# Delta rule of a two-block layer: VectorE instead of GpSimd makes the masked factors of the inverse's levels

## The reference, cut to what matters

```
def step(s, inp):
    r_t, w_t, k_t, v_t, a_t, b_t = inp
    sa = jnp.einsum('bhvk,bhk->bhv', s, a_t)
    s = s * w_t[:, :, None, :] + sa[..., None] * b_t[:, :, None, :] + v_t[..., None] * k_t[:, :, None, :]
    y = jnp.einsum('bhvk,bhk->bhv', s, r_t) if emit else None
    return s, y
```

## Time and profile before

| | |
|---|---|
| median of 3 runs | 3859.14 us (3858.52 to 3877.39) |
| profiled execution | 3855.31 us, of which span 3853.2 us |
| busy over the span | PE 87%, VectorE 62%, ScalarE 49%, POOL 21% |
| stage `rwmix` in the trace | from 785 to 1296 us |
| busy in the stage, 784 to 1292 us | PE 415.5, VectorE 293.5, POOL 301.3, ScalarE 281.6 us of 508 |
| `X` on POOL (line 1428) | 200 instructions, 142.2 us busy, 730 ns each |
| granted TensorE clock in the stage | 0.96 of full speed |

### The profile page before, as it was taken

One profiled execution on the slowest core, in us unless ns is written; L12 is line 12 of the kernel. 1 busy time (PEld: TensorE's weight loads), 2 busy tenths in 40 slices (PEclk: granted clock), 3 DMA queues, 4 the chain that ended last, 5 costly groups with the idle time before them and its releaser, 6 DMA issues. The chain is left out here.

```text
span 3853.2 us, 90173 instructions
## 1 busy us (share of the span) xinstructions
PE 3336.3 (87%) x33247; PEld 2257.5 (59%) x33247; DVE 2376.5 (62%) x4427; ACT 1907.1 (49%) x2993; POOL 823.9 (21%) x1095
## 2 busy tenths in 40 slices
PE   4899799768887597889989989998699999697699
PEld 0899798756766475633323333332377778576577
DVE  1688688845566575537767767776485753076631
ACT  0576567645555343217757767775322221076520
POOL 4000000045566200522212222221222323100000
PEclk6999899879999798989999999999899999898899
DMA  8354444432232437669799999950734223455342
GB/s 317 78 165 160 163 128 142 167 84 59 58 81 62 162 101 252 118 237 321 229 296 349 339 358 343 284 132 6 238 87 120 66 82 104 113 148 128 117 167 77
DMA packets 574272, 639.75 MB, mean 166 GB/s; under 512 B 121312, under 2 KB 485536, under 8 KB 570768
## 3 DMA queue, kind: packets, MB, share of 16 engines
q1 hardware_dynamic: 548576, 564.59, 46.1%
q0 software_dynamic: 25216, 69.34, 7.4%
q10 hardware_dynamic: 48, 0.05, 0.0%
HBM read 489.41 MB, written 161.74 MB: 169 GB/s over the span
## 5 line engine op out<-in xcount | busy, mean ns | idle before, releaser
L2606 PE MATMUL routed_p_gu<-routed_fixed,routed_x 128*32 128x512 f32 x3840 | 569.3, 597 | 0.0
L2606 PE MATMUL routed_p_gu<-moe_exp_w,routed_x 128*32 x1280 | 568.3, 597 | 0.7 <-DVE routed_fixed L2721 0.7
L2721 DVE COPY routed_fixed<-moe_exp_w 128x1024 f32 x640 | 400.8, 683 | 37.5 <-DMA moe_exp_w<-in_exp_w_up_dram 30.4
L2660 ACT COPY routed_fixed<-moe_exp_w 128x1024 f32 x320 | 333.7, 1046 | 134.1 <-PE routed_p_y L2621 83.7
L544 PE MATMUL front_ps<-front_a_high,front_w_high 128*128 128x320 f32 (+1 forms) x1120 | 364.4, 325 | 16.3 <-DVE front_w_low L797 13.3
L544 PE MATMUL front_ps<-front_a_high,front_w_low 128*128 128x320 f32 (+1 forms) x1120 | 355.3, 317 | 0.0
L544 PE MATMUL front_ps<-front_a_low,front_w_high 128*128 128x320 f32 (+1 forms) x1120 | 355.2, 317 | 0.0
L2606 PEld LDWEIGHTS routed_p_gu<-moe_exp_w,routed_x 128*32 128x32 f32 x1280 | 134.9, 110 | 353.6 <-issue 353.6
L2673 ACT COPY routed_fixed<-routed_wd 128x1024 f32 x240 | 235.2, 1043 | 130.1 <-PE routed_p_gu L2606 95.0
L3610 PE MATMUL pre_ps<-pre_a_high,pre_w_high 128*128 128x512 f32 x720 | 287.4, 399 | 14.0 <-ACT pre_xb L3763 7.0
L2621 PE MATMUL routed_p_y<-routed_wd,routed_hT 128*32 x640 | 290.5, 597 | 5.2 <-ACT routed_fixed L2673 5.2
(11 more groups left out here) (541 smaller groups left out, 7466.3 us busy)
## 6 DMA issues: line engine op xcount, KB each, us to landing
moe_exp_w<-in_exp_w_gate_dram SPq DMA_DIRECT2D x64, 1024.0 KB, 11.7
moe_exp_w<-in_exp_w_up_dram SPq DMA_DIRECT2D x64, 1024.0 KB, 15.8
routed_wd<-in_exp_w_down_dram SPq DMA_DIRECT2D x64, 1024.0 KB, 14.7
front_wt<-in_w_in_dram SPq DMA_DIRECT2D x70, 512.0 KB, 4.4
mod_w<-in_w_mod_dram SPq DMA_DIRECT2D x24, 1024.0 KB, 18.2
pre_wt<-in_w_in_dram SPq DMA_DIRECT2D x44, 512.0 KB, 3.9
rw_abrk<-front_rb SPq DMA_DIRECT2D x64, 320.0 KB, 4.9
rwmix_src<-rw_abrk SPq DMA_DIRECT2D x80, 192.0 KB, 2.5
```

Source lines behind the costliest of these rows:

```text
L2606: op = nc.tensor.matmul(p_gu[spot(s), :], x[:, b % 2, k, spot(s)], w, start=(k == 0), stop=(k == KD - 1))
L2660: nc.scalar.copy(fixed[:, place_of(b, c), 0, :], wgu[:, bass.ds(e % WS, 1), c * D:(c + 1) * D].rearrange("p o n -> p (o n)"))\
L2721: op = nc.vector.tensor_copy(fixed[:, place_of(b, c), s - 1, :], wgu[:, bass.ds(es[s] % WS, 1), c * D:(c + 1) * D].rearrange("p o n -> p ( ...
```

## The change

`level(l)`, the multiply of `at` by the mask of level l, is issued by VectorE instead of POOL. Levels 1 to 3 follow in slot `masked`, behind `cc` and one drain; levels 4 and 5 follow VectorE's `W` of `w1` and of `w2`. PE's wait for `x{l}` is now on VectorE's count. POOL keeps `TT`, `faded` and `gate`, and no longer waits for `w1` and `w2`. The instruction's shape, operands and number (200) stay; PE's and ScalarE's instructions and their order stay.

```
-            out = ["keys", "at", "bk", "cc"] + norm[0:1]
+            out = ["keys", "at", "bk", "cc", "x1", "x2", "x3"] + norm[0:1]
             for l in range(1, LEVELS + 1):
-                out += [f"w{l}"] + norm[l:l + 1]
+                out += [f"w{l}"] + ([f"x{l + 3}"] if l < 3 else []) + norm[l:l + 1]
...
-                    PO.wait(pe, by_pool[u], n, f"x{l}")
+                    DV.wait(pe, by_vector[u], n, f"x{l}")
...
+                def level(l):
+                    nc.vector.tensor_tensor(X[u][:, l % 3], at[u][:], consts["rw_mask"][:, MASK_LEVEL + l], ALU.mult)\
+                        .then_inc(by_vector[u], 1)
...
                     op.then_inc(by_vector[u], 1)
+                    dve.drain()
+                    for l in range(1, 4):
+                        level(l)
...
+                    if p in ("w1", "w2"):
+                        level(int(p[1]) + 3)
...
-                    for l in range(1, 4):
-                        level(l)
-                elif p in ("w1", "w2"):
-                    PE.wait(pool, products[u], n, p)
-                    level(int(p[1]) + 3)
```

## The result

The changed kernel takes 3973.24 us (median of 4 runs, 3966.3 to 3978.53) against 3860.43 us before (4 runs, 3858.52 to 3877.39). The ratio is 1.0288, with a 95% interval of 1.027 to 1.0307: 113 us slower. Forecast was 3914 us (59 over the profiled execution before) and a range up to 3945. So the direction was right, and the loss is nearly twice the forecast one and outside the range.

A forecast was written before the change was run, and what follows sets the result against it. It took the stage as bound by chains of handovers between PE, ScalarE and VectorE, no engine full. 40.2 (tiles 1 to 6) + 5.5 (first round) + 13.5 (last three) = 59 us on 3855.3 gave 3914 us, range 3877 to 3945.

The forecast's parts named there:

- Who is waited for: Behind each unit's masked keys PE waits for VectorE's `rest` and `W`; before the multiply by `X` it never waits for POOL.
- A multiply is 0.43 us, three with a drain 1.15: Undisturbed cost on VectorE of one moved multiply, and of the block of levels 1 to 3 behind `cc`.
- The exclusion with `TT`: VectorE's two-SBUF-operand multiplies and POOL's `TT` shut each other out; blocks of 2.1, 1.65, 1.65 and 1.15 us.
- 6.7 us a round, 40.2 in tiles 1 to 6: Added time per middle round: 2.15 + 1.65 + 1.65 + 1.5 - 0.25 over the four units, times six rounds.
- 5.5 us in the first round: Added time in the first round, where the first block has no other unit's work behind it and level 5 hides.
- 13.5 us in the last three rounds: Added time with normalisation between: 4.5 us a round, two of the four blocks costing only 0.3 each.
- Levels 4 and 5 covered except for 0.7 us a round: These multiplies fall into VectorE's idle time, except level 5 of units 1 and 3, paid at 0.35 us each.
- 0.25 us a round back from `faded`: POOL, relieved of the multiplies, makes `faded` earlier for VectorE; credited as -0.25 us a round.
- The step that failed: PE's own times kept unchanged; a clock fall with added idle time named only as making the forecast wrong, without a price.

The follow-up runs named there:

- e1: Changed kernel with the multiplies of levels 1 to 3 taking their first operand from PSUM, times 0, instead of SBUF; 3937.15 us, ratio 1.0184.
- e9: Changed kernel with unread matmuls in PE's idle times in tiles 1 to 6 and also in tiles 7 to 9; 3929.35 us, ratio 1.0173.
- e4: Kernel before with only levels 4 and 5 moved to VectorE, levels 1 to 3 left on POOL; 3882.29 us, ratio 1.0048.
- e7: Kernel before, all levels on POOL, with levels 2 and 3 issued later, in slot t0, so faded goes ahead; 3864.25 us, ratio 0.9993.
- e8: Changed kernel with 10, 10, 7 and 5 unread matmuls a round in PE's four idle times, tiles 1 to 6; 3937.4 us, ratio 1.0184.

## Why the prediction was right about the queue and wrong about PE's own speed

- **Who is waited for.** Right. The idle time of PE is put down to VectorE's `rest` and `W` behind the masked keys, and the list of waits shows it grown, for `rest` from 12.4 to 44.1 us and for `W` from 25.4 to 45.1. In front of the product with `X` it is still `issue` and nobody else (28.2 us in the earlier trace rows, now 34.1). Before:

```profile
PEld rwmix_ps L1251 <- DVE rwmix_rest L1384: 12.4, 24, 1.2
...
PEld rwmix_ps L1231 <- DVE rwmix_W L1379: 25.4, 36, 1.5
```

In the changed kernel:

```profile
PEld rwmix_ps L1251 <- DVE rwmix_rest L1393: 44.1, 24, 3.2
...
PEld rwmix_ps L1231 <- DVE rwmix_W L1386: 45.1, 44, 3.4
...
PEld rwmix_ps L1217 <- issue: 34.1, 160, 0.3
```

- **A multiply is 0.43 us, three with a drain 1.15.** Right: median 0.426, and 1.19 in e1.
- **The exclusion with `TT`.** Right, and a little larger than forecast. Unit 2's block is 2.11 us (2.1 forecast) and unit 0's 1.19 (1.15), but unit 3's is 1.93 and unit 1's 1.71 to 1.96 in tiles 1 to 6, where 1.65 was forecast for each. What the forecast left out is that POOL, now free of `X`, goes on to `faded`, which reads SBUF too: behind unit 3's `cc` of tile 6 the first multiply waits for the end of `TT` and the other two run beside `faded` and take 0.51 us each instead of 0.43.

```profile
1180.34 1.83 DVE L1355 TENSOR_TENSOR rwmix_X<-rwmix_at,rw_mask 128x256 f32<-128x256 f32 x3
...
1180.31 0.72 POOL L1448 TENSOR_TENSOR rwmix_TT<-rwmix_TT,eye 128x256 f32<-128x256 f32 x1
1180.99 0.91 POOL L1460 TENSOR_TENSOR rwmix_faded<-rwmix_S,rwmix_tot 128x64 f32<-128x64 f32 x2
```

  The Trainium skill's rule (SBUF — State Buffer, "Who interferes with whom") covers this case as well: unit 2's third multiply in tile 6 ended at 1166.19, 0.29 us behind POOL's last instruction of `TT` (1165.18 + 0.72), and e1, which has one SBUF operand, doesn't wait.
- **6.7 us a round, 40.2 in tiles 1 to 6.** Right at full clock: e9's rounds 1 to 6 take 320.3 us against 278.8 before, 41.5 more. In part that is luck, since with the blocks as measured the same sum gives about 7.2 us a round.
- **5.5 us in the first round.** 3.6 were measured (50.2 against 46.6).
- **13.5 us in the last three rounds.** Near in two rounds and open in the third. In e9, with the clock at 1.00, tiles 7 and 8 take 61.7 and 58.6 us against 55.9 and 54.2 before: 5.8 and 4.4 more, where 4.5 each were forecast. The last round takes 85.9 against 73.2, 12.7 more, but at a clock of 0.89 where it was 0.99 before. How much of its surplus is clock and how much VectorE's queue is not resolved. All three together are 22.9 us over before.
- **Levels 4 and 5 covered except for 0.7 us a round.** About right: 0.9 in e4 at full clock.
- **0.25 us a round back from `faded`.** Not seen; 2.5 us in all would lie within e7's interval.
- **The step that failed.** The sum moved VectorE's work and left PE's own times as they were. The clock was named only in the last sentence, as something that would make the forecast wrong, with no price and outside the range. What the runs showed in its place is a PE that works at half pace for stretches behind its new waits. That weighs 47 us by the traces (ten rounds 624.0 us in the changed kernel, 576.6 in e9, whose trace is of its fastest run). By the medians it is 44 us for e9 and 36 us for e8, which fills the idle times of six rounds only. The added work costs something too, and e9's last round isn't back at full clock, so the true share may be larger. 59 forecast, 9 more in the late rounds (8 of them in the last) and 47 for the clock make 115, which is the stage's growth.

The trace before the change held the warning. PE was busy 87% of a middle round and in tiles 1 to 6 never stood idle for more than 1.4 us; the forecast itself put 1.15 to 2.1 us on top of each of four waits. The first stretch of the stage, where only one or two units are at work, has the clock at 0.74, and a line of PE's work shows what either level costs: 218 ns for most matmuls, up to 366 at the lower one.

```profile
784.00:836.00 52.00, 36.64 (x845) 29.41 (x846) 20.81 (x58) 21.44 (x63) 25.38 (x47) 0.74 0.40 99
...
L1217 PE MATMUL rwmix_ps<-rwmix_T,rwmix_X x3200: 212/218/366, 793.4 to 1282.2; 64*64 64x64 f32 x189
```

The Trainium skill, TensorE: Matmul & The Clock Gate, section "HAM oscillation — how this bites in real kernels", describes a kernel whose repeated waits let PE's clock drop, so that each burst behind a wait begins slow. This trace agrees, though here it is VectorE that PE waits for: 16 loads take 0.59 us behind a wait of 2.78, and 0.32 where e8 has filled it. It doesn't hold for every wait, as unit 3's block showed.

## What to carry to other kernels

A wait put on a PE that is nearly always busy can be paid twice: once as itself, once as the slower work behind it. Here 6.8 us of new waiting in a round cost 12.7. So ask of every delay how long PE stands still in it, and price PE's next instructions at either clock; whether the clock is the cause can be tested by adding unread work that fits into the gap, with the same work added to the kernel before as the control. And moving work to a faster engine (0.43 against 0.73 us here) loses when the slower one had it beside the path and the faster one has it ahead of what others wait for.

## What the runs showed of the hardware

VectorE's multiplies with both operands in SBUF and POOL's instructions that read SBUF hold each other up also where POOL's instruction uses 64 partitions only. A multiply of 0.43 us took 0.56 and 0.68 us beside POOL's 64x128 instructions (tile 6, from 1164.17 on), 0.97 beside the 128x256 one of line 1448, and 0.51 beside `faded`; POOL's 64x128 instructions of 0.45 us took up to 0.62. With one operand in PSUM three multiplies took 1.09 us in the same place.

The record of PE's granted clock shows two levels, 2.4 and 1.2 GHz. In tiles 1 to 6 of the changed kernel it fell to the lower one 20 times. Those rounds have four idle times of PE's loads each behind the blocks, 1.7, 3.0, 2.8 and 2.2 us in tile 6, and most falls came at or shortly behind one of them; behind some it did not fall. In e8, where the longest idle time of PE in a middle round is 0.7 us, it stayed at the upper level from tile 2 to tile 6. Work that nobody reads made the changed kernel 36 us faster.
